# First up unit of the feed-forward stage: seven combined products in four token quarters replaced by plain products in three token chunks

## The reference

```python
x = x + rms_norm(cross_attention(rms_norm(x, g_pre_x), mem_k, mem_v, w_xq, w_xo), g_post_x)
u = rms_norm(x, g_pre_ffn) @ w_up                    # (1032, 1024) @ (1024, 5632)
c = conv_b + sum(up[:, j:j + L] * conv_w[j] for j in range(3))   # causal over tokens, up = cached rows + u
a, b = split(c, 2)
x = x + rms_norm((silu(a) * b) @ w_down, g_post_ffn)
```

## Time and profile before

| | |
|---|---|
| median of 3 runs | 3143.17 us (3142.03 to 3143.85) |
| the profiled execution's own time | 3146.02 us |
| its span, first to last instruction | 3144.2 us, mean granted clock of TensorE 0.987 |
| busy of the span | PE 95%, DVE 75%, ACT 47%, POOL 42% |
| last part of layer 0's cross attention to the end of up unit 1 | 806 to 914 us |
| the same of layer 1 | 2370 to 2478 us |

### The profile page before, as it was taken

The page is one execution under the profiler, slowest core; times in us unless marked ns, Lnnn a source line. Parts: engine busy times, 40 slices in busy tenths (PEclk is TensorE's granted clock), DMA queues, the critical chain, the costliest instruction groups (busy, mean ns, idle before and its releaser), DMA issues. The chain is left out here.

```text
span 3144.2 us, 62556 instructions
## 1 busy us (share of the span) xinstructions
PE 2994.5 (95%) x25490; PEld 2841.8 (90%) x25490; DVE 2348.5 (75%) x2944; ACT 1486.1 (47%) x2652; POOL 1311.9 (42%) x745
## 2 busy tenths in 40 slices
PE   8999999999889999999999999999997999999997
PEld 8999779988779999999999997899886899999996
DVE  7888763644799999785778877545447999997866
ACT  6453464434445545553445425543434455555532
POOL 1111241112566777664511113301125777775644
PEclk9999999999999999999999999999999999999998
DMA  5112333205533343565421123422164333436654
GB/s 195 50 49 70 92 125 116 88 29 203 174 101 130 134 151 129 197 209 165 151 88 45 57 72 94 164 86 74 34 234 138 106 130 135 155 118 213 204 165 149
DMA packets 188539, 394.55 MB, mean 125 GB/s; under 512 B 13664, under 2 KB 113248, under 8 KB 185696
## 3 DMA queue, kind: packets, MB, share of 16 engines
q1 hardware_dynamic: 187968, 390.50, 37.5%
q10 hardware_dynamic: 288, 0.06, 0.0%
HBM read 307.41 MB, written 77.82 MB: 123 GB/s over the span
## 5 line engine op out<-in xcount | busy, mean ns | idle before, releaser
L345 PE MATMUL ps<-hh,w_hi 128*128 128x258 f32 (+3 forms) x4320 | 1334.4, 309 | 63.0 <-DVE hl L3140 28.4
L346 PE MATMUL ps<-hl,w_hi 128*128 128x258 f32 (+3 forms) x4320 | 1307.5, 303 | 0.0
L347 PE MATMUL ps<-hh,w_lo 128*128 128x258 f32 (+3 forms) x4320 | 1306.8, 303 | 0.0
L345 PEld LDWEIGHTS ps<-hh,w_hi 128*128 128x128 f32 x4320 | 819.4, 190 | 87.8 <-issue 41.9
L330 POOL TENSOR_TENSOR w_lo<-w_raw,w_hi 128x1024 fp32r<-128x1024 f32 x133 | 345.8, 2603 | 1322.4 <-ACT w_hi L322 1322.4
L346 PEld LDWEIGHTS ps<-hl,w_hi 128*128 128x128 f32 x4320 | 820.6, 190 | 2.9
L347 PEld LDWEIGHTS ps<-hh,w_lo 128*128 128x128 f32 x4320 | 819.3, 190 | 0.0
L2386 POOL TENSOR_TENSOR w_lo<-w_raw,w_hi 128x512 fp32r<-128x512 f32 (+1 forms) x168 | 248.3, 1481 | 217.2 <-ACT w_hi L2800 217.2
L2380 POOL TENSOR_TENSOR w_lo<-w_lo_f,w_hi 128x512 fp32r<-128x512 f32 x176 | 259.3, 1493 | 178.6 <-DVE w_lo_f L3169 156.3
L345 PE MATMUL ps<-Y_r,w_hi 128*128 128x258 f32 x1056 | 299.5, 284 | 7.0 <-POOL w_lo L2380 3.7
L346 PE MATMUL ps<-Y_r,w_hi 128*128 128x258 f32 x1056 | 300.1, 284 | 0.0
(11 more groups left out here) (407 smaller groups left out, 5514.1 us busy)
## 6 DMA issues: line engine op xcount, KB each, us to landing
w_raw<-in_w_stream SPq DMA_DIRECT2D x252, 512.0 KB, 3.5
gates<-f_c SPq DMA_DIRECT2D x44, 516.0 KB, 2.7
hl_f<-gates SPq DMA_DIRECT2D x32, 516.0 KB, 5.8
xT<-in_w_stream SPq DMA_DIRECT2D x32, 512.0 KB, 6.9
sums<-xT SPq DMA_DIRECT2D x16, 1024.0 KB, 6.0
w_raw<-sums SPq DMA_DIRECT2D x64, 256.0 KB, 3.3
w_raw<-in_w_stream SPq DMA_DIRECT2D x48, 256.0 KB, 3.4
out_y_cols<-xT SPq DMA_DIRECT2D x6, 1376.0 KB, 8.9
```

The costliest lines, as they stand in the source:

```text
L345: nc.tensor.matmul(out, whi, mhi, start=start, stop=False, skip_group_check=reopened)
L346: nc.tensor.matmul(out, whi, mlo, start=False, stop=False, skip_group_check=reopened)
L347: return nc.tensor.matmul(out, wlo, mhi, start=False, stop=stop, skip_group_check=reopened)
```

## The change

Unit 0 is no longer made of seven products. It is made of the eight plain ones, in the token chunks of the cross attention: `first_step(c, h)` for three chunks c and two column blocks h, each 8 x 3 matmuls of 384, 384 or 264 columns. It takes plain weight blocks (`high_first`, `low_first`; the four `combine_block(0, ...)` are gone) and plain activations, which `normal_x`, `high_of_x` and `low_of_x` make chunk by chunk. Its results leave PSUM by six copies on ACT (`copy_first`); its six `add_out` on DVE are gone. The combined activations T1 to T4 are still made, now for unit 1. `high(P_T1)` and `high(P_T4)` write over plain operands of unit 0, so they wait for the steps of unit 0 that read them. Two means are summed one slab earlier, the operand of chunk 0 is made earlier, and the raw weights of unit 1 are loaded ahead of the store of chunk 2.

```diff
@@ -81,7 +82,12 @@
 
     if n:
         return [(n, c, p) for c in range(NP) for p in range(2)]
-    return [(0, c, p) for p in range(2) for c in range(NP - 1)] + [(0, NP - 1, p) for p in range(2)]
+    return [(0, c, h) for c in range(NCH) for h in range(2)]
+
...
@@ -2319,6 +2339,9 @@
                     load_raw(0, 0)
                     load_raw(0, 1)
                     for c in range(NCH):
+                        if c == NCH - 1:
+                            load_raw(1, 0)
+                            load_raw(1, 1)
...
                     split_lo(pool, FIRST_LOAD[l + 1])
-                    low_block(0, P_11)
-                    low_block(0, P_T1)
-                    low_block(0, P_T2)
-                    low(P_22, A)
-                    low_block(0, P_22)
+                    for q in range(N_FIRST):
+                        low_first(q)
                     low(P_T3, A)
-                    low_block(0, P_T3)
-                    low(P_21, A)
-                    low_block(0, P_21)
+                    low_block(1, P_11)
                     low(P_T4, A)
-                    low(P_22, B)
-                    low_block(0, P_T4)
+                    low_block(1, P_T1)
+                    low_block(1, P_T2)
                     low(P_T3, B)
-                    low(P_21, B)
+                    low_block(1, P_22)
+                    low_block(1, P_T3)
                     low(P_T4, B)
-                    for n in range(FT):
-                        if n:
-                            low_block(n, P_T4)
+                    low_block(1, P_21)
+                    for n in range(1, FT):
+                        low_block(n, P_T4)
                         for k in halves_in(n):
                             sum_half(k)
...
+                    mean(1)
                     unit(1, 6)
                     sample_values(11)
                     sample_values(12)
-                    mean(1)
...
+                    mean(2)
                     unit(2, 0)
-                    mean(2)
+                    def first_step(c, h):
+
+                        at = 2 * c + h
+                        if at >= 4:
+                            wait_first(pe, (at - 4) // 2, h)
+                        for k in range(KT):
+                            rb, kk = divmod(k, 4)
+                            if kk == 0 and c == 0:
+                                pe.wait_ge(f_wlo, 2 * h + rb + 1)
+                            if kk == 0 and h == 0:
+                                pe.wait_ge(f_lo, LO_ORDER.index(("x", c, rb)) + 1)
+                            w = slice(P * kk, P * kk + P)
+                            last = mm3(ps[:, first_bank(c, h), 0:C3[c][1]], ring_block(w_hi, 2 * h + rb, 4)[:, w],
+                                       ring_block(w_lo, 2 * h + rb, 4)[:, w], hh[:, k, cols(c)], hl[:, k, cols(c)], k == 0, k == KT - 1)
+                        last.then_inc(f_step, 1)
...
                     sum_up(4, range(6))
                     unit(2, 7)
                     sum_up(4, (6, 7))
-                    step(0, P_11, A)
+                    first_step(0, 0)
+                    first_step(0, 1)
                     sum_up(5, range(KT))
-                    for c in (P_T1, P_T2, P_22, P_T3, P_21):
-                        step(0, c, A)
-                    for c in (P_11, P_T1, P_T2, P_22, P_T3, P_21):
-                        step(0, c, B)
-                    step(0, P_T4, A)
-                    step(0, P_T4, B)
+                    for c in (1, 2):
+                        first_step(c, 0)
+                        first_step(c, 1)
...
+                    high_first(2)
+                    high_first(3)
                     high(P_T2, A)
                     high(P_T3, A)
-                    copy_out(0, P_11, A)
-                    high_block(0, P_22)
                     squares(2, range(KT))
-                    high_block(0, P_T3)
-                    high_block(0, P_21)
-                    copy_out(0, P_T1, A)
+                    copy_first(0, 0)
+                    high_block(1, P_11)
+                    copy_first(0, 1)
+                    root(5)
+                    high_block(1, P_T1)
+                    high_of_x(2, 0)
+                    high_of_x(2, 1)
+                    copy_first(1, 0)
+                    copy_first(1, 1)
+                    high(P_T1, A)
                     high(P_T4, A)
-                    root(5)
-                    copy_out(0, P_T2, A)
-                    for c in (P_11, P_T1, P_22, P_T2, P_T3):
-                        high(c, B)
-                    copy_out(0, P_11, B)
-                    high_block(0, P_T4)
-                    high(P_21, B)
+                    high(P_T2, B)
+                    high(P_T3, B)
+                    copy_first(2, 0)
+                    copy_first(2, 1)
+                    high(P_T1, B)
+                    high_block(1, P_T2)
+                    high_block(1, P_22)
                     high(P_T4, B)
...
+                        copy_out(n, P_11, A)
+                        copy_out(n, P_11, B)
+                        if n == 1:
+                            high_block(1, P_T3)
+                            high_block(1, P_21)
+                            start_conv(0, 0)
+                        high_block(n, P_T4)
+                        copy_out(n, P_T1, A)
+                        copy_out(n, P_T1, B)
+                        if n == 1:
+                            start_conv(0, 1)
+                        silu(n - 1)
+                        copy_out(n, P_T2, A)
+                        copy_out(n, P_T2, B)
...
+                    def normal_x(c, h):
+                        for k in range(4 * h, 4 * h + 4):
+                            last = nc.vector.scalar_tensor_tensor(Y[:, k, cols(c)], xT[:, k, cols(c)], gT[:, l, G_PRE_FFN + k:G_PRE_FFN + k + 1],
+                                                                  rs[:, cols(c)], ALU.mult, ALU.mult)
+                        last.then_inc(f_h, 1)
+
                     add(("post", 1, 4))
                     adds(0, range(4, KT))
                     add(("post", 1, 5))
+                    scale_of(1)
+                    normal_x(0, 0)
                     add(("post", 1, 6))
-                    scale_of(1)
+                    normal_x(0, 1)
...
+                    def low_of_x(c, h):
+
+                        dve.wait_ge(f_chi, HI_ORDER.index(("x", c, h)) + 1)
+                        at = (slice(None), rows_of(h), cols(c))
+                        nc.vector.tensor_tensor(hl[at], Y[at], hh[at].bitcast(F32), ALU.subtract).then_inc(f_lo, 1)
...
                         nc.vector.tensor_tensor(C[:, 1, :], C[:, 0, :], C[:, 1, :], ALU.mult).then_inc(f_g, 1)
 
-                    dve.wait_ge(w_used, VISIT[l, "xo", xo_slab(2 * KT - 1), 1] + 1)
-                    scale_of(1)
-                    operand_of_x(P_11, A)
-                    operand_of_x(P_21, A)
+                    low_of_x(0, 0)
+                    low_of_x(0, 1)
                     scale_of(3)
-                    operand_of_x(P_T1, A)
-                    operand_of_x(P_22, A)
-                    combine(P_T1, A)
-                    combine(P_T2, A)
-                    combine(P_T3, A)
-                    for c in (P_T1, P_T2, P_22, P_T3):
-                        combine_block(0, c)
-                    low(P_11, A)
+                    normal_x(1, 0)
+                    normal_x(1, 1)
+                    low_of_x(1, 0)
+                    low_of_x(1, 1)
+                    for c in (P_T1, P_T2, P_T3):
+                        combine(c, A)
                     normalise(4)
                     residual(2)
-                    low(P_T1, A)
                     combine(P_T4, A)
                     low(P_T2, A)
-                    dve.wait_ge(w_used, VISIT[l, "xo", xo_slab(3 * KT - 1), 2] + 1)
+                    combine_block(1, P_T1)
                     scale_of(5)
-                    operand_of_x(P_11, B)
-                    operand_of_x(P_T1, B)
-                    operand_of_x(P_22, B)
+                    normal_x(2, 0)
+                    normal_x(2, 1)
+                    low_of_x(2, 0)
+                    low_of_x(2, 1)
                     combine(P_T1, B)
                     combine(P_T2, B)
+                    low(P_T1, A)
                     combine(P_T3, B)
-                    low(P_11, B)
-                    operand_of_x(P_21, B)
+                    combine_block(1, P_T2)
+                    combine(P_T4, B)
+                    combine_block(1, P_22)
                     low(P_T1, B)
-                    combine(P_T4, B)
                     low(P_T2, B)
-                    for p in (A, B):
-                        for c in (P_22, P_T3, P_21):
-                            add_out(0, c, p)
-                    for c in (P_T1, P_T2, P_22, P_T3):
-                        combine_block(1, c)
+                    combine_block(1, P_T3)
```

(35 more changed lines are left out.)

161 lines of the change are left out of this document (86 added, 75 removed).

## The result

The changed kernel takes 3123.55 us (median of 4 runs, 3122.41 to 3125.25) against 3143.06 for the kernel before in the same session: a ratio of 0.9939, 95% interval 0.9921 to 0.9956. That is 19.5 us faster; 24 were forecast, and the range held it. The profiled execution has a span of 3123.4 us at a mean clock of 0.986 (before: 3144.2).

What follows compares the result with a forecast made beforehand. PE, busy 95% of the span, was taken as the bound. Per layer +2.7 for matmuls, -22.2 for unit 0's waits and low clock, +7.4 for unit 1's new waits: 12.1 us gained, 24 for two, 3119 us; range 3111 to 3124.

Steps and rivals of the forecast that it cites:

- Start of unit 0: Layer 0: `first_step(0, 0)` starts at 839.5 us, bounds 838.5 and 842, against 841.57 for the end of the sums.
- Matmuls of unit 0: Unit 0: 168 matmuls of 258 columns (19.9 us) replaced by 96 of 384 and 48 of 264, 22.6 us; cost +2.7.
- x of chunk 2: Before the last sum of squares: DVE has it ready at 852.6, against 849.4 before; PE waits 847.9 to 853.0.
- Sum at low clock: Last sum of squares, behind PE's wait: 16 matmuls at low clock, 5.03 us for 14 plus 0.1, to 858.1.
- Tail: Unit 1: DVE's 13.3 and POOL's 13.2 us take turns, 26.5 us from 865.0; `conv(0, 0)` ends 891.5, 892.4 with waits.
- The choice of 902.0 between the bounds: End of unit 1, taken as 902.0 between 899.4 (three POOL pieces behind the conv) and 903.8, nearer to the latter.
- The full sum by turns: Unit 1 ends at 903.8 if DVE and POOL take turns fully, including 1.2 us of low clock behind the wait.
- Units behind unit 1 "begin as they did": Units 2 to 10 begin as before, so the gain stays 914.1 - 902.0 = 12.1 us per layer.
- The tail is not hidden: Denies the rival of a hidden tail in unit 1: unit 1 ends near 896, -18 per layer, 3107 us; chance 0.20.
- It does not reach into unit 2: Denies the longer-tail rival: late DVE work costs three to six us more per layer, 3127 to 3130; chance 0.21.
- The raw weights were not late: Denies rival "slower": unit 1's raw weights landing after 855 delay the tail one for one, deciding from 867; chance 0.04.

Runs made afterwards that it cites:

- second profile: The changed kernel itself run again as a control, nothing edited: 3124.7 us, ratio 0.9941 to the kernel before.
- The run with POOL held back: Changed kernel, with POOL's last quarter-B operand and last two weight blocks of unit 1 waiting until DVE finished the first conv: 3129.6 us.
- weights that landed at 861: Changed kernel, with raw weights of unit 1 loaded behind the last store of x instead of ahead of it: 3125.0 us.
- the adds ahead: Changed kernel with both ACT copies ahead, and DVE adding P_22 and P_T3 of unit 1 before the first conv: 3129.0 us.
- ACT's order twice: Changed kernel with P_T1's copies ahead of three roundings and the conv's start on ACT, 3124.7 us; then also silu behind P_T2's copies, 3124.9 us.
- the kernel with the filler: Changed kernel plus 24 matmuls of chunk 0, repeated and overwritten, before the last sum of squares: 3119.4 us, ratio 0.9922.

## Why the prediction was right, and where not

Times are counted from the anchor (the prediction's less 805.05).

*Start of unit 0*: forecast 34.4, measured 35.8. The cause is what the text named as possible, ACT's new copies holding up the weight splits: two waits for them, 1.20 and 0.68, where one of 0.4 had been. Within its bounds.

*Matmuls of unit 0*: chunk 0 took 8.6 us and chunks 1 and 2 14.4, without a wait inside either; 22.6 forecast, 23.0 measured.

*x of chunk 2*: 47.5 forecast, 48.2 measured. The wait before the sum, 4.25, is of the size said (5.1). *Sum at low clock*: 16 matmuls in 6.25 us, 5.1 forecast. The price came from a stretch granted 0.66; here the grant was 0.53, and the second profile of the same kernel has 4.82 us for 14 of them where this one has 6.17: a like wait did not fix the price. Together unit 0 ended at 69.4 in place of 67.3.

*Tail*: the strongest step. The sum of DVE's and POOL's work was put at 27.4 us with the waits; from 868.06 to the conv's end at 894.65 are 26.6. The Trainium skill (SBUF — State Buffer, section "SBUF: two separate sides") calls the shared port of these two an exclusive lock. The run with POOL held back agrees: `conv(0, 0)` came 4.2 us earlier (3.6 in layer 1) for three pieces of POOL, 4.4 us by their own lengths, taken out of its way.

*The choice of 902.0 between the bounds* is the step that failed. Unit 0 gained 17.3 us of the 19.5 forecast, and unit 1 took 9.6 us more than before where 7.4 were priced. The full sum by turns gave 903.8 (98.8 from the anchor) and I took 1.8 off for turns that overlap; measured are 101.35. Of the 2.6 us between the full sum and the measurement, the tail's start (62.2 for 60.0: x and the sum of squares) is +2.3, its length -0.8, the rest of unit 1 behind `P_T3` +1.1: 11.0 us in place of 9.9, since 24 matmuls from 896.17 ran at a granted 0.50 and cost more than the 1.2 us set aside. PE's waits in unit 1 were 7.1 us, not some 10, since it came to them later and at a lower clock.

*Units behind unit 1 "begin as they did"* was wrong to our gain. The kernel before still had waits of 1.1 us in 914 to 1050, the longest of them this one, in unit 2:

```profile
932.39 0.36 PE L345 MATMUL ps<-f_t,w_hi 128*128 128x258 f32 x1 [0.84 <-DVE f_u L3176]
```

The changed one has none there, so that 7.7 us at the start of unit 2 are 8.8 at unit 3 (9.1 in layer 1). Both layers make 18.0. The spans differ by 20.8; behind the two units 3 another 3.6 us are gained, and 0.8 were lost ahead of the first anchor. Half a microsecond per layer is the wait for DVE's adds at the end of the up units (3.8 and 4.0 for 4.3 and 4.6). The rest is open. (There are 22 up units in a layer, as the 22 gates in the trace show, not the 11 of the text ahead; no number hung on it.)

*The time fell into the range by luck.* With the prediction's own premise, that nothing changes behind unit 1, the 7.7 and 8.0 us of this trace give 3143.2 - 15.7 = 3127.5, outside 3111 to 3124 (by the second profile, 9.7 and 7.9, it is 3125.6). It took what was not forecast, the waits gone from unit 2 and the microseconds that are open, to bring 3123.55, half a microsecond inside the upper end. What holds of the forecast is the mechanism: DVE's waits go, and two waits for ACT behind a tail of turns pay back a part.

*Rivals.* The tail is not hidden. It does not reach into unit 2: PE has no wait from 907 to 1050 us. The raw weights were not late, and weights that landed at 861 moved the tail by about a microsecond.

*What the experiments add*: unit 3 starts when the last operands, the combined blocks of units 1 and 2, the conv, the gate and the adds have passed through DVE, and this work begins with the last root. (The end of unit 1 alone is not so bound: with the adds ahead it came 9 us earlier.) Putting only the wait of PE elsewhere, by ACT's order twice, by POOL's and by DVE's, left unit 3 within 0.7 us of where it was or made it later. What brought the last root earlier helped, by 4 to 5, 3.6 and 2 to 3.4 us per layer.

## What to carry to other kernels

When PE waits for different engines in turn, look for the one queue behind all these names, and move its start, not the wait: here the last chunk's scaling, which a few lines in another order brought 4.7 us forward. Price a tail in which two engines take turns as the sum of their work: here 26.5 us by the rows, 26.6 measured. Measure a reordering one stage further on than where it gains: the one that brought unit 2 nine microseconds forward lost them all by unit 3.

## What the runs showed of the hardware

PE's clock has a price that can be bought back with useless work: with 24 matmuls thrown away in front of it, the sum took 3.35 us at a granted 1.00 in both layers, against 4.82 to 6.17 in the four passages of the changed kernel behind a wait of 4.3 us. A wait of 3.3 us alone doesn't fix what follows. Behind the wait at `P_22` the 24 matmuls ran at a granted 0.65 in the changed kernel, but these are the same stretches, behind the same wait, in the kernel with the filler and in the second profile of the changed kernel itself:

```profile
885.60:888.60 3.00, 3.00 (x24) 2.90 (x24) 2.96 (x2) 2.55 (x3) 3.00 (x2) 1.00 0.00 0
886.99:890.00 3.01, 3.01 (x24) 2.90 (x24) 2.98 (x2) 2.55 (x3) 3.01 (x2) 1.00 0.00 0
```

In layer 1 of the kernel with the filler the grant there was 0.63 again. So the difference is not one of the edit, and what decides it is not shown. In both traces the saving was spent at the next wait, 5.22 and 5.20 us in place of 3.78. The same program run again ended unit 0 of layer 0 at 68.1 in place of 69.4 from the anchor: such differences of one trace are no effect of an edit.
